# Splitting the opening loads of a two-block transformer kernel over SyncE's and ScalarE's queues, and reordering them

## What is computed

```python
h = rmsnorm(x, norm_gain[layer])
proj = h @ w_in_ab[j]
qa, ka, va, ga, qb, kb_, vb_, gb, fb = split_cols(proj, AB_SIZES)   # 8 panels of 512 columns, then 8 gate columns
qa = rmsnorm(to_heads(qa, MOBA_HEADS), moba_q_gain[j])
ka = rmsnorm(to_heads(ka, MOBA_HEADS), moba_k_gain[j])
ya = from_heads(moba_attention(qa, ka, to_heads(va, MOBA_HEADS), moba_slopes))
qb = rmsnorm(to_heads(qb, FOX_HEADS), fox_q_gain[j])
kb_ = rmsnorm(to_heads(kb_, FOX_HEADS), fox_k_gain[j])
log_f = jax.nn.log_sigmoid(fb.astype(jnp.float32) + b_forget[j].astype(jnp.float32)).transpose(0, 2, 1)
yb = from_heads(fox_attention(qb, kb_, to_heads(vb_, FOX_HEADS), log_f))
y = jnp.concatenate([ya * jax.nn.silu(ga), yb * jax.nn.silu(gb)], axis=-1)
x = x + y @ w_out_ab[j]
```

## Time and profile before

| | us |
|---|---|
| three runs | 1066.44, 1068.68, 1064.13 |
| median | 1066.44 |
| the profiled execution, its own time | 1057.87 |
| its span in the profile | 1056.1 |
| PE busy | 1001.9 (95%) |
| DVE, ACT busy | 629.7 (60%), 547.2 (52%) |
| mean granted TensorE clock | 0.978 of full speed |

### The profile page before, as it was taken

How to read it: one execution, slowest core, us unless ns; L and a number is a source line. 1 busy time by engine, 2 the same in 40 slices (tenths; PEclk the granted TensorE clock), 3 DMA queues, 4 the chain that set the end, 5 groups by cost and what they waited for, 6 DMA issues and landing times.

```text
span 1056.1 us, 15751 instructions
## 1 busy us (share of the span) xinstructions
PE 1001.9 (95%) x6172; PEld 887.1 (84%) x6172; DVE 629.7 (60%) x1216; ACT 547.2 (52%) x1029; POOL 34.0 (3%) x83
## 2 busy tenths in 40 slices
PE   9899999998798988997999999999999989999997
PEld 7678778786686888986999999899989869999996
DVE  5687554584864456746764554556883557645554
ACT  6485554555574345645554444454663456544442
POOL 4011000000010000000000000000000000000000
PEclk9999989999898999999999999999999999999999
DMA  7885313454331334352455655657435515555551
GB/s 242 224 194 112 120 41 120 159 189 131 99 130 42 97 104 130 121 159 81 157 173 188 200 185 176 238 164 193 145 99 171 184 53 192 182 180 196 191 188 40
DMA packets 114167, 158.14 MB, mean 150 GB/s; under 512 B 13783, under 2 KB 55085, under 8 KB 114093
## 3 DMA queue, kind: packets, MB, share of 16 engines
q1 hardware_dynamic: 113804, 156.60, 48.0%
q10 hardware_dynamic: 288, 0.52, 0.1%
HBM read 156.06 MB, written 1.05 MB: 149 GB/s over the span
## 4 chain that ended last, share of the span: by engine, by line
PE 83%; DVE 7%; ACT 4%; issue 3%; SPq 2%; DMA 1%; DVEq 0%; ACTq 0%
PE bank L474 24%; PE bank L475 24%; PE bank L476 24%; PE bank L612 2%; PE bank L637 2%; DVE w_lo L1701 2%; PE bank L528 2%; PE bank L626 1%; PE bank L606 1%; SPq L2362 1%; ACT w_hi L1229 1%; ACT pb L1393 1%; SPq L2367 1%; DMA raw<-in_w_in_ab 1%; PE bank L591 1%
## 5 line engine op out<-in xcount | busy, mean ns | idle before, releaser
L1701 DVE TENSOR_TENSOR w_lo<-raw,w_hi 128x1024 fp32r<-128x1024 f32 (+2 forms) x292 | 335.3, 1194 | 194.0 <-ACT w_hi L1229 193.4
L1229 ACT CAST w_hi<-raw 128x1024 fp32r<-128x1024 f32 (+2 forms) x292 | 282.9, 1026 | 153.2 <-DMA raw<-in_mlp_w_in 77.4
L474 PE MATMUL bank<-xT_hi,w_hi 128*128 128x256 f32 x784 | 224.6, 286 | 2.7 <-DVE xT_lo L1758 1.8
L476 PE MATMUL bank<-xT_hi,w_lo 128*128 128x256 f32 x784 | 222.9, 284 | 0.0
L475 PE MATMUL bank<-xT_lo,w_hi 128*128 128x256 f32 x784 | 222.9, 284 | 0.0
L474 PE MATMUL bank<-w_hi,xT_hi 128*128 128x512 f32 (+1 forms) x432 | 165.1, 382 | 3.1 <-DVE xT_lo L1756 2.3
L475 PE MATMUL bank<-w_lo,xT_hi 128*128 128x512 f32 (+1 forms) x432 | 160.6, 372 | 0.0
L476 PE MATMUL bank<-w_hi,xT_lo 128*128 128x512 f32 (+1 forms) x432 | 160.3, 371 | 0.0
L474 PEld LDWEIGHTS bank<-xT_hi,w_hi 128*128 128x128 f32 x784 | 151.4, 193 | 4.4 <-issue 2.6
L475 PEld LDWEIGHTS bank<-xT_lo,w_hi 128*128 128x128 f32 x784 | 151.3, 193 | 0.6
L476 PEld LDWEIGHTS bank<-xT_hi,w_lo 128*128 128x128 f32 x784 | 151.3, 193 | 0.0
(11 more groups left out here) (242 smaller groups left out, 1097.2 us busy)
## 6 DMA issues: line engine op xcount, KB each, us to landing
raw<-in_mlp_w_in SPq DMA_DIRECT2D x32, 1024.0 KB, 5.4
raw<-in_mlp_w_out SPq DMA_DIRECT2D x32, 1024.0 KB, 5.1
raw<-in_w_in_ab SPq DMA_DIRECT2D x13, 1024.0 KB, 9.4
raw<-in_w_in_cd SPq DMA_DIRECT2D x13, 1024.0 KB, 5.0
raw<-in_xa_w_kv SPq DMA_DIRECT2D x8, 1024.0 KB, 5.4
raw<-in_sb_w_qkv SPq DMA_DIRECT2D x16, 512.0 KB, 5.2
raw<-in_w_out_ab SPq DMA_DIRECT2D x4, 1024.0 KB, 5.1
raw<-in_w_out_cd SPq DMA_DIRECT2D x4, 1024.0 KB, 5.1
```

The lines of the kernel that those rows point to most:

```text
L474: pe.matmul(o, wh, ih, start=start, stop=False, skip_group_check=True)
L476: return pe.matmul(o, wl, ih, start=False, stop=stop, skip_group_check=True)
L1229: nc.scalar.copy(w_hi[:, u % SLOTS, a], raw[:, u % SLOTS, a]).then_inc(hi_ready, 1)
L1701: V.tensor_tensor(w_lo[:, u % SLOTS, a], raw[:, u % SLOTS, a], w_hi[:, u % SLOTS, a].bitcast(F32), ALU.subtract).then_inc(lo_ready, 1)
```

## The change

ScalarE issues nine of the fifteen small gain loads at the head of its stream, between its table load and its first wait. SyncE keeps six of them; the gate columns move from behind unit 4 to behind unit 6. Unit 5 still stands behind the gain vectors left on SyncE and ahead of the four loads of constants.

```diff
+ACT_LOADS = 10
...
             nc.scalar.preload_act_table_set("natural_log_exp_and_others")
+            for r0, n, ap in gain_loads[1:ACT_LOADS]:
+                o = stage[r0:r0 + n, :]
+                act.dma_start(o if len(ap.shape) == 2 else o.rearrange("p (h d) -> p h d", h=2), ap).then_inc(stage_in, 16)
             act.wait_ge(*read_of("gains0"))
             start()
...
             for u in range(PIECED, SLOTS):
                 weight(u)
-            f_cols = A["w_in_ab"][0].rearrange("(c p) n -> p c n", p=P)[:, :, 8 * PANEL:8 * PANEL + HEADS]
-            sp.dma_start(f_raw[:, :, :], f_cols).then_inc(fox_in, 16)
-            for load in gain_loads[1:]:
+            for load in gain_loads[ACT_LOADS:]:
                 gain_rows(*load)
             weight(SLOTS)
             sp.wait_ge(setup_ready, 1)
...
             for o, i_ in loads:
                 sp.dma_start(o, i_).then_inc(small_in, 16)
-            for u in range(SLOTS + 1, names["qb", 0]):
+            weight(SLOTS + 1)
+            f_cols = A["w_in_ab"][0].rearrange("(c p) n -> p c n", p=P)[:, :, 8 * PANEL:8 * PANEL + HEADS]
+            sp.dma_start(f_raw[:, :, :], f_cols).then_inc(fox_in, 16)
+            for u in range(SLOTS + 2, names["qb", 0]):
                 weight(u)
             sp.dma_start(mem[:, :, :], tok(A["mem_2"])).then_inc(mem_in, 16)
```

## The result

| | before | changed |
|---|---|---|
| median of 20 runs each, us | 1064.82 | 1058.01 |
| lowest and highest, us | 1057.77, 1070.02 | 1050.11, 1063.09 |
| profiled execution, own time, us | 1057.87 | 1060.67 |
| its span, us | 1056.1 | 1058.9 |
| its mean granted clock | 0.978 | 0.971 |

The changed kernel takes 0.9934 of the time before, with an interval of 0.9914 to 0.9953: some 7.0 us less (5.0 to 9.2; the medians differ by 6.8), where 5.6 were forecast.

A forecast was written before the change was run, and what follows sets the result against it. PE bounds the kernel, with a stall at qa's transposes from unit 5's late issue: 5.84 − 0.2 = 5.6 us off the median, 1066.44 − 5.6 = 1060.8. The range was 1058.5 to 1065.5.

The forecast's parts named there:

- What bounds the kernel: Opening: PE, 95% busy, idles 4.27 us ahead of qa's transposes because SP issues unit 5 late, at 28.49.
- What goes, 4.27 + 1.57: At qa's transposes: PE's 4.27 us idle and 1.57 us of slow clock behind it vanish, together 5.84 us.
- Issued at 16.0 and as fast as before it lands at 22.9: Unit 5's load: earlier issue, same transfer time, leaving the transposes' input ready 4.1 us ahead of PE.
- It has to land by 31.1: Unit 5's deadline for qa's transposes: PE's arrival at 39.36 less 8.27 us from landing to transposes.
- It must land by 47.8: Unit 7's deadline, from PE taking it at 52.1; issued at 27.7 it lands by 45.0.
- The case that I priced at 1.0 us: Rival, new wait for unit 7: issue blocked behind the gate columns, landing 48.8, 1.0 us late, total 1061.8; chance 0.07.
- What is added, 0.2: Nine DMA issues on ACT ahead of its first CAST cost 0 to 0.24 us, taken as 0.2.
- Shared issuing: Rival at the start: SP and ACT take turns, ACT's nine issues last 8.7 us, total 1064.1 to 1065.5; chance 0.37.
- The rule weighed against the sum: Skill's rule that several issuing engines save only usually small issue time; by it the gain would be near nothing.
- No issue of ACT was blocked: Rival: one ACT issue stands 6.09 us, first CAST 6.3 us late, total 1066.9, with sharing 1071.5; chance 0.06.
- unit 5 was in time: Rival: SP's remaining small loads stand 2.4 us each, unit 5 lands after 31.1, up to 1066.4; chance 0.05.
- the runs lie up to 2.3 us from their median: Run spread, subtracted from the forecast 1060.8 to give the range's low end, 1058.5.

The follow-up runs named there:

- the seven traces named above: Traces with nine loads on ScalarE and x where it was; the transposes of x's right half start at 15.2 to 15.8 us in them.

## Why the prediction came out as it did

**What bounds the kernel: right.** The stall was unit 5's late issue. Holding the unit back brought it back (4.01), moving it forward took it away.

**What goes, 4.27 + 1.57: right**, though the hundredths are partly luck. From one set of transposes to the other it takes 6.33 or 6.34 us in the six later traces in which PE comes to ka's transposes without a wait, the changed kernel's second among them. Its first has 6.43, so 0.1 us of standing hides there, and the slow clock cost 8.00 − 6.33 = 1.67. To it came 0.77, since PE's matmuls follow each other at 0.23 us from 10.9 on and not from 13.1. I had not counted it, and the change did not buy it: in the second trace of the same kernel they came at that pace from the first, 2.34 us were lost to x instead, and ka's transposes were only 51.63 − 47.09 = 4.54 us earlier than in the kernel before.

**"Issued at 16.0 and as fast as before it lands at 22.9": the first half right, the second wrong.** The issue came at 16.65, the landing at 29.4. The 6.87 us of the earlier trace rows were taken while the DMA engines were 10% busy, after SP had left them idle; the changed kernel keeps them full (1.05 from 18 to 27, at 339 GB/s), and a unit issued then lands behind all that is under way. The 4.1 us of slack were 0.95.

**"It has to land by 31.1" (unit 5): right for qa, wrong for ka.** I gave ka's chain only unit 6 as its start, but on ACT and DVE it also stands behind qa's. Ka's transposes start no earlier than 15.6 us after unit 5's CAST, so for PE's arrival in the changed kernel (38.59 + 6.33 = 44.92) unit 5 had to land by 29.3, and it landed at 29.37: hence the 0.1. Landings at 30.45 and 30.78, both ahead of 31.1, cost 0.70 and 0.85 us at ka. The term of the sum stood, with 0.1 us to pay and not with slack.

**"It must land by 47.8" (unit 7): wrong.** I followed unit 7 to PE's own use of it and not to what stands behind its CAST in ACT's order. The real deadline is 42.3. It held by 0.8 us in the changed kernel, and unit 7's CAST waited too long for its transfer in three of the experiments, with waits of PE of 4.58, 2.52 and 1.74 behind it. The case that I priced at 1.0 us, unit 7 landing at 48.8, would by this deadline have cost 6.5. It didn't happen: unit 7's own issue took 1.75 us behind the gate columns.

**What is added, 0.2: right.** No cost shows: the first CAST starts at 5.82, 5.87 before. The issues do run beside the table load.

**Shared issuing, chance 0.37: refuted.** ACT's nine issues lasted 0.24 to 0.70 us each, 4.34 together, where the rival wanted 8.7. Nor did SP pay: its eight pieces took 4.44 to 5.13 us beside ACT's issues, and 4.09, 4.85 and 5.01 in the three traces with no issue on ACT there (the kernel before and two experiments). The rule in the Trainium skill, "Perfetto Trace Analysis", section "DMA Instruction — HWDGE (DVE, Sync)", that the descriptor block is locked for one sequencer at a time would make two queues take turns; the trace does not agree for SP and ACT, as far as whole issues go: both queues show issues of usual length in the same microseconds. Turns too short to show beside the spread of SP's eight pieces are not excluded. The rule weighed against the sum, from the Trainium skill, "DMA: Bandwidth & Descriptors", section "Issuing engines are not separate DMA queues", holds in that another engine saves issue time alone. Of one load this time is small here too (0.4 us, where unit 5 took 6.9 to land), but sixteen loads in a row had 16.15 us of it, and taking it away from ahead of unit 5 was worth about 6 us. It need not be another engine that does it: by order alone the ratio came to 0.9929.

**The other rivals.** No issue of ACT was blocked; no new wait came for unit 7, though with 0.8 us left it was nearer than its chance of 0.07 said; unit 5 was in time but for 0.1 us. The forecast's mechanism was the one that happened.

**The number and the range: this is the step that failed.** It is not the gain: 5.6 were forecast, and 7.0 [5.0, 9.2] measured do not exclude it. It is the term "the runs lie up to 2.3 us from their median", taken for all the uncertainty at the low end, with a median of three runs, 1066.44, as the start. Twenty runs of the kernel before have their median at 1064.82 and spread over 12.3 us, twenty of the changed one over 13.0; and medians move as well: 1064.64, 1066.31 and 1067.63 for the kernel before in the later comparisons, 1051.78 for the changed kernel in its second trial of six runs. Of the 2.8 us between 1060.8 and 1058.01, 1.6 are the starting median; the other 1.2, by which the gain was larger, cannot be told from none. The profiled execution had given the hint: at 1057.87 it lay 8.6 us under the median, outside the three runs, and I noted it and then left it out of the range. With a range that took in this spread, 1058.01 would have been well inside. And the chance of "faster" was held down by shared issuing, for which the earlier trace rows spoke less than I let it.

## What to carry to other kernels

When a queue's order is changed, follow each load to the instruction that waits for it, and then to everything that stands behind that instruction in its engine's order: the deadline that binds is the earliest of theirs. Follow a chain of results likewise into the next one that runs on the same engines: here qa's norm chain set when ka's could start. A transfer's time taken from a stretch where the DMA engines idle does not hold once the change fills them. And before a gain of half a per cent is predicted or read from two profiles, compare the granted clock by stretch: what it differs by far from the edit is not the edit's.

## What the runs showed of the hardware

**The granted clock differs from one execution of a kernel to the next.** The two traces of the changed kernel are the clearest pair: 0.88 and 0.94 from 284 to 400, 61.4 and 42.0 us at the lower level in all, spans of 1058.9 and 1049.7. Over its 20 runs time and mean clock go together: the fastest, 1050.11 us, had 0.981, the slowest, 1063.09, had 0.967. 0.014 of some 1050 us is 14.7 us, and the difference is 13.0, so the clock by itself is large enough to make the whole spread of this kernel's times. That it does is read from the two going together; no run held the clock fixed. Why the same instructions are granted more slow clock in one execution than in another stays open: the stretches do not begin at the same time, but no run here took that as its question.

**A slow pace that the granted clock does not show.** In nine of the fourteen traces the first matmuls follow each other at 0.43 us, nearly twice their later 0.23, while the granted clock stands at 1.00 (in the kernel before 1.00 from 7 to 13 us, with the slow pace until 13.1). It ended between 1.8 and 5.7 us after the first of them; in the other five traces there was none. Three small matmuls ahead of them went with none once and with the two shortest, 1.8 us, twice, which is no proof: the changed kernel itself had 3.1 us of slow pace in one trace and none in the other. Where the pace was fast from the start, PE stood 1.6 to 2.3 us for x's right half. With the slow pace this wait was at most 0.6, so most of the slow pace is hidden behind the transfer, but not all: in the kernel before, PE came to these transposes at 15.90 without a wait, 0.2 to 0.7 us later than in the seven traces named above.

**Two queues issuing at once** cost nothing that shows beside the spread between traces (SP's eight pieces: 4.44 to 5.13 us with ACT issuing, 4.09 to 5.01 without), and issues on ACT run beside its table load (issues from 0.75, the load from 0.72 to 2.00).

**Some issues stand for long.** Behind the gate columns with their 1024 short runs, the next load stood for 6.09 us in the kernel before and for 3.18 with nine loads on ScalarE; unit 7's issue behind them took 0.37 to 3.42 us in the traces that have it there. The gate columns are not needed for it: norm_mix took 2.16 us behind unit 4 in the experiment that moved them alone. The same kinds of load take 0.4 us elsewhere. I think of it as the queue waiting for room, but no run measured that room.

**With the DMA engines full, the issue no longer sets the landing.** Unit 5 took 6.9 us when issued into idle engines (28.49, 10% busy). Issued at 15.2, 16.65 and 21.44, it landed at 29.74, 29.37 and 30.45.
